# Adding the last two expert slot tiles by products instead of by a store and gathers

## The reference

```python
combine = jnp.sum(jax.nn.one_hot(expert_id, N_EXPERTS, dtype=jnp.float32) * ew[..., None], axis=1)
y = jnp.zeros_like(t)
for e in range(N_EXPERTS):
    he = jax.nn.silu(t @ w_gate[e]) * (t @ w_up[e])      # 1024 -> 512
    y = y + combine[:, e:e + 1] * (he @ w_down[e])       # 512 -> 1024
...
x = x + hierarchical_moe(...)
return rms_norm_2(x, g_final)
```

## Time and profile before

| | |
|---|---|
| profiled execution, its own time | 2305.15 us |
| its span, first to last instruction | 2303.1 us |
| TensorE busy | 2215.6 us (96%) |
| VectorE busy | 1299.9 us (56%) |
| ScalarE busy | 1107.0 us (48%) |
| mean granted TensorE clock | 0.986 |

### The profile page before, as it was taken

One profiled execution on the slowest core, in us unless ns is written; L12 is line 12 of the kernel. 1 busy time (PEld: TensorE's weight loads), 2 busy tenths in 40 slices (PEclk: granted clock), 3 DMA queues, 4 the chain that ended last, 5 costly groups with the idle time before them and its releaser, 6 DMA issues.

```text
span 2303.1 us, 30060 instructions
## 1 busy us (share of the span) xinstructions
PE 2215.6 (96%) x10999; PEld 1811.4 (79%) x10999; DVE 1299.9 (56%) x1911; ACT 1107.0 (48%) x1642; POOL 52.5 (2%) x70
## 2 busy tenths in 40 slices
PE   9999999999999999999999999999999799999994
PEld 7887788888888876788888888868888678888883
DVE  4556663333374446653333467642554579899995
ACT  3425363433432238362432444473344278888884
POOL 1000000000000000000000000000000010000001
PEclk9999999999999999999999999999999799999997
DMA  6220233333323320243333333203222299999994
GB/s 194 83 74 28 83 119 93 99 96 95 101 74 101 92 74 1 92 129 100 92 100 95 97 101 99 89 20 101 88 86 82 71 379 411 411 412 412 411 409 187
DMA packets 129137, 338.57 MB, mean 147 GB/s; under 512 B 10528, under 2 KB 11712, under 8 KB 129040
## 3 DMA queue, kind: packets, MB, share of 16 engines
q1 hardware_dynamic: 117744, 296.85, 36.7%
q0 software_dynamic: 7840, 27.59, 3.6%
q10 hardware_dynamic: 3456, 12.81, 1.4%
HBM read 320.96 MB, written 16.25 MB: 146 GB/s over the span
## 4 chain that ended last, share of the span: by engine, by line
PE 88%; DVE 7%; ACT 3%; DMA 1%; issue 1%; POOL 0%; SPq 0%; DVEq 0%; ACTq 0%; POOLq 0%
PE bank L2271 42%; PE bank L2274 18%; PE bank L2681 11%; PE bank L2718 6%; PE bank L2344 2%; PE bank L2353 2%; PE bank L2410 1%; PE bank L2295 1%; DVE w_l L1345 1%; PE bank L2368 1%; PE bank L2661 1%; PE bank L2333 0%; ACT w_h L821 0%; DVE stat L1377 0%; PE bank L2668 0%
## 5 line engine op out<-in xcount | busy, mean ns | idle before, releaser
L1345 DVE TENSOR_TENSOR w_l<-w_raw,w_h 128x1024 fp32r<-128x1024 f32 x370 | 447.4, 1221 | 555.3 <-ACT w_h L821 551.7
L821 ACT CAST w_h<-w_raw 128x1024 fp32r<-128x1024 f32 x370 | 385.6, 1050 | 728.0 <-PE bank L2271 511.1
L2271 PE MATMUL bank<-w_h,xt_h 128*128 128x512 f32 (+1 forms) x960 | 376.4, 392 | 7.1 <-DVE w_l L1345 2.6
L2271 PE MATMUL bank<-w_h,xt_l 128*128 128x512 f32 (+1 forms) x960 | 371.4, 387 | 0.0
L2271 PE MATMUL bank<-w_l,xt_h 128*128 128x512 f32 (+1 forms) x960 | 371.0, 386 | 0.0
L2271 PE MATMUL bank<-w_h,ht_h 128*128 128x512 f32 x624 | 244.0, 391 | 0.7 <-DVE w_l L1345 0.7
L1345 DVE TENSOR_TENSOR w_l<-spare,w_h 128x1024 fp32r<-128x1024 f32 x184 | 220.5, 1218 | 41.6 <-ACT w_h L821 40.9
L2271 PE MATMUL bank<-w_h,ht_l 128*128 128x512 f32 x624 | 242.9, 389 | 0.0
L2271 PE MATMUL bank<-w_l,ht_h 128*128 128x512 f32 x624 | 242.8, 389 | 0.0
L2274 PE MATMUL bank<-xt_h,w_h 128*128 128x512 f32 x608 | 236.8, 389 | 3.4 <-ACT arena L961 2.4
L2274 PE MATMUL bank<-xt_h,w_l 128*128 128x512 f32 x608 | 236.6, 389 | 0.0
(11 more groups left out here) (351 smaller groups left out, 2908.4 us busy)
## 6 DMA issues: line engine op xcount, KB each, us to landing
w_raw<-in_ffn_w_dram SPq DMA_DIRECT2D x128, 512.0 KB, 3.7
spare<-in_w_down_dram SPq DMA_DIRECT2D x92, 512.0 KB, 10.9
spare<-in_w_gate_dram SPq DMA_DIRECT2D x88, 512.0 KB
w_raw<-in_w_up_dram SPq DMA_DIRECT2D x88, 512.0 KB, 11.0
w_raw<-in_w_in_dram SPq DMA_DIRECT2D x30, 512.0 KB, 3.7
w_raw<-in_ev_w_in_dram SPq DMA_DIRECT2D x28, 512.0 KB, 3.7
w_raw<-in_od_w_in_dram SPq DMA_DIRECT2D x24, 512.0 KB, 3.7
slot_y_dram<-slot_out ACTq DMA_DIRECT2D x23, 512.0 KB, 6.7
```

The source lines that it names most:

```text
L821: nc.scalar.copy(w_h[:, n % SLOTS, :], raw_of(n)).then_inc(sem("w_hi"), 1)
L1345: V.tensor_tensor(w_l[:, s_, :], raw_of(n), w_h[:, s_, :].bitcast(F32), ALU.subtract)\
L2271: mm = T.matmul(bank[set0 + m][:, 0:g.width], a[:, c, toks_of(m)], b[:, kk, :], start=first, stop=last)
```

## The change

`slot_y` has rows for 21 tiles only, and tiles 21 and 22 are no longer stored. GpSimd's last gathers wait for the stores of tiles 19 and 20. The two late tiles reach the tokens by products:

- Behind the routing, VectorE marks the pairs of token and expert that lie in tiles 21 and 22 (`late`), makes their shares (`shares`) and a diagonal matrix for each (`DIAG`, 128x2048). TensorE makes each late slot's share from them (8 fp32 products of 2 columns), and selection matrices `PICK`, one of 128x128 for each token tile and late tile (8 products of 256 columns, banks 3 and 4). The four unread products are gone.
- In tile 0, ScalarE copies `PICK` out of PSUM, and so that the banks are free the slots of tile 1 are transposed after gate piece 1 instead of after up piece 1. VectorE sets the shares and slots of late pairs to zero (5 operations).
- ScalarE runs a Silu on one element ahead of the experts and a square root on one element at the end.
- The down product of tile 21 has the transposes of tile 22's hidden values in its middle; the hidden values of tile 22 go to a buffer of their own, its down product to banks 5 and 6.
- ScalarE scales both outputs by the slots' shares. TensorE adds, for each token tile, `PICK` times output 21 (two fp32r products a half, high and low part) and `PICK` times output 22 (one fp32 product a half). For token tile 3, the gathered row of k = 1 is added by an fp32 product with a diagonal of shares as well. VectorE adds the banks to `X` (`picked_up`).

The diff without its guards, default arguments and renamed tile numbers; in order: constants, GpSimd, ScalarE, VectorE, TensorE.

```diff
-SLOT_TILES = 2 * S // P + N_EXPERTS - 1
+TILES = 2 * S // P + N_EXPERTS - 1
+SLOT_TILES = TILES - 2
...
-        down_last = plan.place(tile_groups()[2:])
+        down_last = plan.place([slot_group("down", wd, (5, 6))])
...
+        LATE = (TILES - 2, TILES - 1)
+        quarters_h, quarters_l = (v[:, :, :].rearrange("p c s -> p (c s)").rearrange("p (r n) -> p r n", r=4) for v in XT)
+        PICK = quarters_h[:, 2, :].rearrange("p (i l s) -> p i l s", i=NT, l=2)
+        HID_LAST = [quarters_h[:, 3, HALF * k:HALF * (k + 1)].rearrange("p (c s) -> p c s", c=4) for k in range(2)]
+        DIAG = xt_l[:, 4:8, :].rearrange("p c s -> p (c s)").rearrange("p (j s) -> p j s", s=P)
+        Y_LATE = [quarters_l[:, 2, :], slot_out[:, 1, :]]
+        Y_LATE_LOW = quarters_l[:, 3, :]
+        Y_BANK = (3, 5)
+        SUM_BANK = (0, 3, 5, 0)
...
-            for last in (SLOT_TILES - 2, SLOT_TILES - 1):
+            for last in (LATE[0] - 2, LATE[0] - 1):
...
+            own.do(nc.scalar.activation(gated[:, 0:1], eps1, ACT.Silu))
...
+            act.wait_ge(sem("late_product"), 1)
+            nc.scalar.copy(late_share, bank[7][:, 256:258]).then_inc(sem("late_copy"), 1)
...
+            def late_hi(k, g):
+                for half in range(2):
+                    act.wait_ge(sem("bank_full"), g.b + half + 1)
+                    if k:
+                        act.wait_ge(*moved("y_stored", LATE[0] - 2, None))
+                    nc.scalar.activation(Y_LATE[k][:, half * HALF:(half + 1) * HALF], bank[Y_BANK[k] + half][:, :],
+                                         ACT.Copy, scale=late_share[:, k:k + 1]).then_inc(sem("late_copy"), 1)
...
+                    if j == 2 and t_ == 0:
+                        slots_hi(1, 0)
+                        slots_hi(1, 1)
...
+                if i is None and t_ == 0:
+                    act.wait_ge(sem("late_product"), 2)
+                    nc.scalar.copy(PICK.rearrange("p i l s -> p (i l s)"),
+                                   banks[:, 3:5, :].rearrange("p b n -> p (b n)")).then_inc(sem("late_copy"), 1)
...
-            hidden_hi(SLOT_TILES - 1)
-            down_tile(down_last[0], SLOT_TILES - 1)
+            for j in range(4):
+                split(tile_22[2].n + LOOK + j, None, 0)
+                if j == 2:
+                    hidden_hi(TILES - 1, dst=HID_LAST[0])
+            split(down_last[0].n + LOOK, None, 0)
+            late_hi(0, tile_22[2])
+            own.do(nc.scalar.activation(ms[:, 8:9], eps1, ACT.Sqrt))
+            act.wait_ge(sem("slots_known"), 1)
+            nc.scalar.activation(gated[:, 0:P], ident, ACT.Copy, scale=share[:, 1, NT - 1:NT]).then_inc(sem("late_copy"), 1)
+            late_hi(1, down_last[0])
...
-            V.tensor_copy(slot_of[:, :, :].rearrange("p k t -> p (k t)"), slot_f).then_inc(sem("slots_known"), 1)
...
-            for j in range(LOOK):
+            late, shares, early = rt(452, 2 * NT, 2), rt(492, 2 * NT, 2), rt(468, 2 * NT)
+            flat_share = share.rearrange("p k t -> p (k t)")
+            for k in range(2):
+                own.mark(V.tensor_scalar(late[:, :, k], tile_f, float(LATE[k] + 1), None, ALU.is_equal))
+            own.wait()
+            V.tensor_tensor(shares, late, flat_share.unsqueeze(2).to_broadcast([P, 2 * NT, 2]), ALU.mult)\
+                .then_inc(sem("late_value"), 1)
+            split(first_expert_piece, None, 0)
+            V.tensor_tensor(DIAG, ident.unsqueeze(1).to_broadcast([P, 4 * NT, P]),
+                            rt(452, 4 * NT).unsqueeze(2).to_broadcast([P, 4 * NT, P]), ALU.mult)\
+                .then_inc(sem("late_value"), 1)
+            for j in range(1, LOOK):
...
+                    if j == 2 and t_ == 0:
+                        slots_lo(1, 0)
+                        slots_lo(1, 1)
...
+                if i is None and t_ == 0:
+                    dve.wait_ge(sem("late_value"), 1)
+                    own.do(V.tensor_tensor(early, late[:, :, 0], late[:, :, 1], ALU.add))
+                    own.do(V.tensor_scalar(early, early, -1.0, 1.0, ALU.mult, ALU.add))
+                    own.mark(V.tensor_tensor(flat_share, flat_share, early, ALU.mult))
+                    own.do(V.tensor_tensor(slot_f, slot_f, early, ALU.mult))
+                    V.tensor_copy(slot_of[:, :, :].rearrange("p k t -> p (k t)"), slot_f).then_inc(sem("slots_known"), 1)
...
+            def late_lo():
+                for half in range(2):
+                    dve.wait_ge(sem("late_copy"), half + 3)
+                    cols = slice(half * HALF, (half + 1) * HALF)
+                    V.scalar_tensor_tensor(Y_LATE_LOW[:, cols], bank[Y_BANK[0] + half][:, :], late_share[:, 0:1],
+                                           Y_LATE[0][:, cols].bitcast(F32), ALU.mult, ALU.subtract)\
+                        .then_inc(sem("late_value"), 1)
...
-            hidden_lo(SLOT_TILES - 1)
-            for g in down_last:
-                split_for(g)
+            for j in range(4):
+                split(tile_22[2].n + LOOK + j, None, 0)
+                if j == 2:
+                    hidden_lo(TILES - 1, hid=HID_LAST)
+            split(down_last[0].n + LOOK, None, 0)
...
+            dve.wait_ge(sem("late_copy"), 1)
+            def gathered(i):
+                dve.wait_ge(sem(f"back{i}"), 32)
+                own.mark(V.scalar_tensor_tensor(X[:, i, :], back[:, i, 0, :], share[:, 0, i:i + 1], X[:, i, :],
+                                                ALU.mult, ALU.add))
+                if i < NT - 1:
+                    own.wait()
+                    own.mark(V.scalar_tensor_tensor(X[:, i, :], back[:, i, 1, :], share[:, 1, i:i + 1], X[:, i, :],
+                                                    ALU.mult, ALU.add))
+            def picked_up(i):
+                own.wait()
+                dve.wait_ge(sem("late_product"), i + 3)
+                V.tensor_tensor(X[:, i, :], X[:, i, :],
+                                banks[:, SUM_BANK[i]:SUM_BANK[i] + 2, :].rearrange("p b n -> p (b n)"), ALU.add)\
+                    .then_inc(sem("final_x"), 1)
             def normalised(i):
...
-            for i in range(NT):
-                dve.wait_ge(sem(f"back{i}"), 32)
-                own.do(V.scalar_tensor_tensor(X[:, i, :], back[:, i, 0, :], share[:, 0, i:i + 1], X[:, i, :],
-                                              ALU.mult, ALU.add))
-                V.scalar_tensor_tensor(X[:, i, :], back[:, i, 1, :], share[:, 1, i:i + 1], X[:, i, :],
-                                       ALU.mult, ALU.add).then_inc(sem("final_x"), 1)
-                if i:
-                    normalised(i - 1)
+            late_lo()
+            gathered(0)
+            gathered(1)
+            picked_up(0)
+            gathered(2)
+            picked_up(1)
+            normalised(0)
+            picked_up(2)
+            gathered(3)
+            picked_up(3)
+            normalised(1)
+            normalised(2)
...
-            for _ in range(4):
-                T.matmul(bank[4][:, :], ident, X[:, 0, 0:HALF], start=True, stop=True)
+            pe.wait_ge(sem("late_value"), 1)
+            pe.wait_ge(sem("tokens_known"), 1)
+            for j in range(2 * NT):
+                mm = T.matmul(bank[7][:, 256:258], in_place[:, j, :].bitcast(F32), r_tmp[:, 492 + 2 * j:494 + 2 * j],
+                              start=j == 0, stop=j == 2 * NT - 1)
+            mm.then_inc(sem("late_product"), 1)
             def slots_transposed(t_, i=None):
...
+                if t_ == 0:
+                    slots_transposed(1)
...
-            def down_product(g, t_, i=None):
-                pe.wait_ge(sem("m_lo"), of_tile(1, 1, t_, i))
-                if t_:
-                    pe.wait_ge(sem("m_out"), of_tile(2, 0, t_, i))
-                for j in range(4):
+            def down_product(g, t_, i=None, js=range(4), hid=(hid_h, hid_l)):
+                if js[0] == 0:
+                    pe.wait_ge(sem("m_lo"), of_tile(1, 1, t_, i))
+                    if t_ == 0:
+                        pe.wait_ge(sem("late_copy"), 2)
+                    if t_ and g.bank[0] == 3:
+                        pe.wait_ge(sem("m_out"), of_tile(2, 0, t_, i))
+                for j in js:
...
+            pe.wait_ge(sem("late_value"), 2)
+            for i in range(NT):
+                for k in range(2):
+                    j = k * NT + i
+                    mm = T.matmul(bank[3 + i // 2][:, 2 * P * (i % 2):2 * P * (i % 2) + 2 * P], in_place[:, j, :],
+                                  DIAG[:, 2 * j:2 * j + 2, :].rearrange("p l s -> p (l s)"), start=k == 0, stop=k == 1)
+            mm.then_inc(sem("late_product"), 1)
...
-            hidden_transposed(SLOT_TILES - 1)
-            down_product(down_last[0], SLOT_TILES - 1)
+            down_product(tile_22[2], LATE[0], js=(0, 1))
+            hidden_transposed(LATE[1])
+            down_product(tile_22[2], LATE[0], js=(2, 3))
+            down_product(down_last[0], LATE[1], hid=HID_LAST)
+            def first_late(i):
```

(25 more changed lines are left out.)

50 lines of the change are left out of this document (26 added, 24 removed).

## The result

The changed kernel took 2288.83 us in the median of 4 runs (2287.37 to 2290.68); the kernel before, beside it, 2304.57 (2302.95 to 2308.02, 4 runs). The ratio is 0.993, with a 95% interval of 0.9914 to 0.9946: 15.7 us saved where 13.5 were forecast. In 6 later runs the same kernel took 2290.8 (2288.6 to 2293.65), ratio 0.9938 [0.9923, 0.9953].

A forecast was written before the change was run, and what follows sets the result against it. TensorE, busy 96% of the span, was taken to bound the kernel, with a serial tail behind it. 13.1 us at the end plus 0.4 at the start, off 2305.15, gave 2291.6; range of 8 in 10: 2288.8 to 2297.0.

The forecast's parts named there:

- the mechanism of the end: Tail: TensorE's idle goes, store and gathers leave the path, VectorE's additions follow with one wait; 13.1 us earlier.
- the start's term: From the first slot gather to tile 1: table load moved, against added work and a cold clock; net 0.4 us gained.
- Rival E: End: the change does less than it says, tile 22's hidden values still stop TensorE; 2294 to 2295.5 us; chance 0.05.
- One remark: End: with fp32 products of 1.0 us instead of 0.85, VectorE waits 1.3 us more in all.
- the cold stretch: TensorE's slow matmuls around 2265, behind the 2.1 us idle; said to go with that idle, 1.8 us.
- I take until 1857: Start: TensorE's clock stays low 7 us after the transposes begin, slowing seven gate matmuls; 1.4 us lost.
- My term for the table load: Start: the first Silu's table load, on the chain between up pieces, moves to idle time; 1.28 us.
- The own range: Whole time: 2290 to 2294 us, from the fp32 product, the clock at the start and the stores.
- A: Start: the clock stays cold; cold to 1864 makes the time 2294.5 us; chance 0.12.
- B: TensorE's tail runs cold from 2268.75; time 2302.9 us, no change, or about 2297 if half cold; chance 0.06.
- D: Experts' first tiles: the clock stays at the lower level, slower than before; cold to 1900 gives 2313 us; chance 0.03.
- C: End: gathers or stores are late by contention, with 8 us in hand; say 2295 us; chance 0.05.

The follow-up runs named there:

- e3: Changed kernel with output 22 added by one fp32r product a half instead of an fp32 one, its low part left out: 2289.62 us.
- e8: Changed kernel with token tile 3's second gathered row added on VectorE, without the products with the diagonal of shares: 2290.86 us.
- e2: Changed kernel with GpSimd's last gathers also held until tile 21's down product is done: 2293.84 us.
- e1: Changed kernel with tile 22's hidden values evacuated one piece later and transposed behind tile 21's whole down product: 2290.99 us.
- e10: The kernel before once more, nothing edited: 2305.2 us.
- e9: The changed kernel once more, nothing edited: 2290.8 us.
- e4: Kernel before with a one-column Silu on ScalarE ahead of the first splits, so its table loads early: 2302.78 us against 2305.44.
- e11: Changed kernel without the one-column Silu ahead of the experts: 2288.76 us.
- e6: Changed kernel with three unread fp32 products back behind the ranking and one behind the late slots' product: 2288.19 us.

## Why the prediction was right, and where it was wrong

The profiled span was forecast at 2289.6 us (2290.0 - 0.4) and measured 2285.5, so 4.1 us lower. Of these the end holds 0.3, the start 0.8 and the code that both kernels share 3.0. So the mechanism of the end was right, and two steps failed: the start's term was sized too small, and the shared code was put at nothing.

**The end: right in mechanism and size.** Idle 0 between the two down products; `first_late` 5.53 us behind `down_last`'s start (24 x 0.233 = 5.6). The fp32 product was taken at 0.85 and measured 0.86, the one wait at 0.5 and measured 0.42, the span's rest 3.1 and measured 3.1. The term was 13.1; the first two profiles give 96.86 - 83.50 = 13.4. e3 and e8 confirm what sets the end (VectorE), e2 the 5 us of cover for the first pair of gathers. The stores cost nothing extra. Rival E's price was too high: with the idle back, e1 lost 1.6 us, not 2.4 to 3.9. One remark does not add up: by the prediction's own terms an fp32 product of 1.0 us costs VectorE 1.15 us more, not 1.3. Nothing hangs on it.

**The cold stretch counted in full: too much.** The step "and with them the cold stretch (1.8 us)" read one execution. The stretch occurs in two of four. Its size was also too large: 7.42 us holds the longer first spacing and the whole last matmul, and 24 x 0.233 does not. From the same start to the same end the warm case took 5.87 (e10), so the stretch is 1.5 us, of which 1.2 show at the kernel's end. Over the four profiles the end before is 96.4 on the mean, and the gain 12.9.

**The start: the term that was mis-sized.** In the first two profiles the stretch gained 1.2 us (356.68 - 355.46) where 0.4 stood. Over all profiles (six with the changed start on the mean 355.78, two of before 356.48) it gained 0.7. The failed step is "I take until 1857, 7 us after the transposes begin, so seven gate matmuls cost 0.2 more each: 1.4": it was 5.0 us, and three to four matmuls were slow, which is 0.7 us. Put on a common first gather, gate began at +8.44 (I had +8.62), and tile 1's transposes were forecast at +25.47 and came at +24.57 and +25.15.

The step was also put on a path where it did not count. In the six profiles with the changed start the clock was up 3.4 to 5.6 us behind the transposes' start, and tile 1's transposes do not follow it: +24.83 where it came first (e3), +24.80 where it came last (e8). In e3 the gate matmuls stand 0.23 to 0.26 apart from the first one on:

```profile
1854.99 0.42 PE L2785 MATMUL bank<-w_h,xt_h 128*128 128x512 f32 x1
1855.25 0.40 PE L2785 MATMUL bank<-w_l,xt_h 128*128 128x512 f32 x1
```

So the clock was up before any 512-column product had run there. The prediction had read it as lifted by those. The Trainium skill, "TensorE: Matmul & The Clock Gate", section "What's actually happening", says that the moment of the rise varies from run to run; these six profiles agree. The 0.6 us between the two profiles of one kernel (e9 and the first) is something else: the clock rose 10.0 us behind the first gather in both. What TensorE waited for ahead of those transposes, 0.53 to 1.18 us in all six, was VectorE's `value`. VectorE stood behind ScalarE's casts there, and ScalarE waited for the landing of tile 1's pieces (1.40 us in the first profile, 1.73 in e9). That landing I did not count at all. This is why the early Silu, worth about 1 us in the kernel before (e4), is worth at most 0.5 in the changed one (e11). My term for the table load, its whole 1.28 us, was too large, and the one for the cold clock too. The two errors offset each other in part.

**The range: too narrow at its low end.** The own range of 2290 to 2294 named three sources, "the fp32 product, the clock at the start, the stores". It put the code that both kernels share at nothing. Between the two first profiles that code differs by 3.0 us: 0.6 up to the router's last passes, and 2.45 in them. Over all fourteen profiles the start of these passes differs by 5.6 us (1819.62 to 1825.22), for a reason that was not looked for. So the runs of one kernel spread over 5 us and more: 2300.24 to 2310.35 for the 17 of before. A median of four or five runs can then lie 1 to 2 us off.

**What stays open.** The stretches that the change touches give 12.9 + 0.7 = 13.6, against the 13.5 forecast. The first comparison gave 15.7 and the second 14.3, and 13.6 lies within both intervals. But chance is a weak account of the rest. Every experiment with the changed kernel has a comparison of its own; with what its stretches lost or won put back, the ten comparisons give 14.3 to 17.9 us. By the five sets of runs of the kernel before they give 15.7, 15.3, 17.5, 15.2 and 15.4, all above 13.6. Each of these alone is uncertain by some 3 us; together they speak for about 2 us more than the profiled stretches show. The shared code does not hold it in the profiles: up to the end of the router's last passes the four with the kernel before's code took 1827.1 us on the mean, and the ten with the changed kernel's 1827.1. The four profiles with the kernel before's end may show it too fast; one of them (e10) was the fastest of its twelve runs. That was not tested, and the cause stays open.

**The rivals.** A (start cold for long), B (tail cold) and D (slower) did not occur: the clock is up from about 1852.1 at the start, and in every window from 2248 to 2280 at the end. C: the gathers held the 5 us that were worked out, and stores took 2.6 to 2.7 to land. E: no idle at the hidden values.

No version was found that is measurably faster than the change. e3 gains 0.4 us by dropping a low part; e6 gains nothing that shows.

## What to carry to other kernels

Before you sum against a profile, compare two profiles of the same kernel stretch by stretch, between marks that both share. What differs there without an edit is the width of your range, and a stretch of it that your change would "save" (here the cold 1.5 us) counts only as often as it occurs. If several comparisons all miss your stretches by the same sign, they may hold something that your few profiles do not show. An early load of an activation table, or a warm clock, is worth what the next resource leaves of it: here the landing of weights took over as soon as the engines came earlier. A serial tail of store, gather and add can be replaced by a product with a selection matrix. Then the adding engine sets the end, and each addition there counts in full.
